# Three norm borders of a two-block transformer kernel: the first unit pair behind each border multiplies rows that have no norm factor yet

## The reference

```
for l in range(DEPTH):                       # DEPTH = 2
    h = rms_norm(x, norm_mix[l])
    z = h @ w_in[l]                          # 2560 columns
    ... attention, gated recurrence and convolution over parts of z ...
    x = x + mix @ w_out[l]
    h = rms_norm(x, norm_mlp[l])
    x = x + jnp.square(jax.nn.relu(h @ w_mlp_in[l])) @ w_mlp_out[l]   # 4096 wide

def rms_norm(x, g):
    y = x * rsqrt(mean(x * x, axis=-1) + EPS)
    return y * g
```

## Time and profile before

| what | value |
|---|---|
| median of 3 runs | 3816.25 us |
| lowest and highest | 3813.84 and 3819.67 us |
| profiled execution | span 3819.2 us from first to last instruction; no time of its own is given for it |
| PE busy | 3654.5 us, 96% |
| DVE busy | 2094.7 us, 55% |
| ACT busy | 1377.0 us, 36% |
| mean granted TensorE clock | 0.974 |

### The profile page before, as it was taken

How to read it: one execution, slowest core, us unless ns; L and a number is a source line. 1 busy time by engine, 2 the same in 40 slices (tenths; PEclk the granted TensorE clock), 3 DMA queues, 4 the chain that set the end, 5 groups by cost and what they waited for, 6 DMA issues and landing times.

```text
span 3819.2 us, 47920 instructions
## 1 busy us (share of the span) xinstructions
PE 3654.5 (96%) x19016; PEld 2946.7 (77%) x19016; DVE 2094.7 (55%) x2735; ACT 1377.0 (36%) x1839; POOL 867.3 (23%) x716
## 2 busy tenths in 40 slices
PE   8988999998899999999899999999989999989998
PEld 6667888766788878886677888788868778778887
DVE  5867443487744454456666435633564655665334
ACT  4764332276433232123663222322233334332222
POOL 2211655321065536552223620000000000000000
PEclk8999999999999999998999999999999999999999
DMA  5212555431265546663234643233322222222331
GB/s 148 78 40 71 149 147 139 100 78 42 68 151 146 137 115 160 145 144 74 52 77 102 162 118 94 77 101 98 99 71 79 72 65 85 63 65 80 101 95 67
DMA packets 564249, 377.75 MB, mean 99 GB/s; under 512 B 37297, under 2 KB 561162, under 8 KB 564026
## 3 DMA queue, kind: packets, MB, share of 16 engines
q1 hardware_dynamic: 564026, 374.69, 37.1%
HBM read 372.45 MB, written 2.17 MB: 98 GB/s over the span
## 4 chain that ended last, share of the span: by engine, by line
PE 79%; DVE 14%; ACT 4%; issue 3%; SPq 0%; DMA 0%; DVEq 0%; ACTq 0%
PE bank L447 62%; PE bank L455 3%; DVE conv_sum L1250 2%; PE bank L493 2%; DVE w_lo L425 2%; PE bank L866 1%; PE bank L487 1%; PE bank L488 1%; DVE norm_tmp L1709 1%; DVE std L928 1%; PE bank L2347 1%; ACT w_hi L416 1%; DVE norm_tmp L1703 1%; DVE X L1705 1%; DVE H_lo L1715 1%
## 5 line engine op out<-in xcount | busy, mean ns | idle before, releaser
L447 PE MATMUL bank<-H_hi,w_hi 128*128 128x512 f32 x2384 | 968.3, 406 | 5.0 <-DVE w_lo L425 1.8
L447 PE MATMUL bank<-H_hi,w_lo 128*128 128x512 f32 x2384 | 932.4, 391 | 0.0
L447 PE MATMUL bank<-H_lo,w_hi 128*128 128x512 f32 x2384 | 931.6, 391 | 0.0
L425 DVE TENSOR_TENSOR w_lo<-w_raw,w_hi 128x2048 fp32r<-128x2048 f32 (+3 forms) x285 | 657.1, 2306 | 148.4 <-ACT w_hi L416 140.7
L416 ACT ACTIVATE w_hi<-w_raw 128x2048 fp32r<-128x2048 f32 (+3 forms) x285 | 529.1, 1857 | 306.4 <-DMA w_raw<-in_ffn_w_up 131.3
L447 PEld LDWEIGHTS bank<-H_hi,w_hi 128*128 128x128 f32 x2384 | 448.3, 188 | 140.6 <-issue 49.0
L526 POOL TENSOR_TENSOR w_mod_raw<-w_mod_raw,silu_c 128x1024 f32<-128x1024 f32 x144 | 283.8, 1971 | 1185.7 <-DMA w_mod_raw<-in_w_mod 1139.6
L447 PE MATMUL bank<-U_hi,w_hi 128*128 128x512 f32 x1376 | 539.4, 392 | 3.7 <-DVE note L985 3.7
L447 PE MATMUL bank<-U_hi,w_lo 128*128 128x512 f32 x1376 | 535.8, 389 | 0.0
L447 PE MATMUL bank<-U_lo,w_hi 128*128 128x512 f32 x1376 | 535.6, 389 | 0.0
L447 PEld LDWEIGHTS bank<-H_hi,w_lo 128*128 128x128 f32 x2384 | 448.1, 188 | 96.7 <-issue 0.3
(11 more groups left out here) (368 smaller groups left out, 4681.1 us busy)
## 6 DMA issues: line engine op xcount, KB each, us to landing
w_mod_raw<-in_w_mod SPq DMA_DIRECT2D x576, 128.0 KB, 5.7
w_raw<-in_ffn_w_gate SPq DMA_DIRECT2D x88, 512.0 KB, 4.0
w_raw<-in_ffn_w_up SPq DMA_DIRECT2D x88, 512.0 KB, 5.5
w_raw<-in_dil_w_in SPq DMA_DIRECT2D x36, 1024.0 KB, 5.1
w_raw<-in_w_mlp_in SPq DMA_DIRECT2D x32, 1024.0 KB, 6.0
w_raw<-in_w_mlp_out SPq DMA_DIRECT2D x32, 1024.0 KB, 5.5
w_raw<-in_ffn_w_down SPq DMA_DIRECT2D x32, 1024.0 KB, 5.0
w_raw<-in_w_in SPq DMA_DIRECT2D x16, 1024.0 KB, 5.5
```

Of the source, the lines that this page charges most:

```text
L425: dve.eng.tensor_tensor(WL[u % SLOTS][:, 0:n], RAW[u % SLOTS][:, 0:n], WH[u % SLOTS][:, 0:n].bitcast(F32), ALU.subtract).then_inc(lo_done. ...
L447: mm = pe.eng.matmul(bank[0:m, :], w[:, k, c0:c0 + m], r[:, k, :], start=(k == 0 and i == 0), stop=(k == kt - 1 and i == 2))
```

## The change

At the three borders, while the last tiles are added to `X`, ACT makes `H_hi` from `X * g` without the factor (`raw_high`) and DVE `H_lo` (`raw_low`). TensorE runs the first pair on these (`pe_raw_pair`) and does the sums of squares behind its third k-step and the spread of the factor behind its fourth. DVE copies the factor out of the bank (`FACTORS`), scales all eight tiles, and ACT and DVE write `H_hi` and `H_lo` again in place, each tile once TensorE has read it (`raw_gone`). The four output tiles of the pair get the factor as DVE reads them out of their banks: for `up` together with the relu, for `z0` in a plain multiplication; ACT did these four before. The units behind the pair wait for the rewritten tiles one by one.

```
+        def pe_raw_pair(pe, u):
...
+            for _, _, place, turn in todo:
+                pe.eng.wait_ge(acc_free[place].sem, turn - 1)
+            for k in range(DT):
+                pe.eng.wait_ge(part_hi.sem, part_hi.next(pe))
+                for wh, wl, place, _ in todo:
+                    pe.eng.matmul(banks[place][:], wh[:, k], rh[:, k, :], start=(k == 0), stop=False)
+                    pe.eng.matmul(banks[place][:], wl[:, k], rh[:, k, :], start=False, stop=False)
+                pe.eng.wait_ge(rhs_ready.sem, rhs_ready.next(pe))
+                for wh, wl, place, _ in todo:
+                    mm = pe.eng.matmul(banks[place][:], wh[:, k], rl[:, k, :], start=False, stop=(k == DT - 1))
...
+                if k == RAW_SUMS:
+                    pe_running_sums(pe)
+                if k == RAW_SPREAD:
+                    pe_spread(pe)
...
+        def raw_high(act, t, gain):
+            act.eng.activation(HH[:, t, :], X[:, t, :], ACT.Identity, scale=gain(t)).then_inc(part_hi.sem, part_hi.add())
...
+        def raw_low(dve, t, gain):
+            dve.eng.wait_ge(part_hi.sem, part_hi.next(dve))
+            dve.eng.scalar_tensor_tensor(HL[:, t, :], X[:, t, :], gain(t), HH[:, t, :].bitcast(F32), ALU.mult, ALU.subtract).then_inc(rhs_ready.sem, rhs_ready.add())
...
+        def scaled_act(act, u):
+            act_std(act, D, True)
+            split_hi(act, u + 2)
+            for t in range(DT):
+                act.eng.wait_ge(scaled.sem, scaled.next(act))
+                raw_gone(act, u, t)
+                act.eng.activation(HH[:, t, :], SC[t % 2][:], ACT.Copy).then_inc(part_hi.sem, part_hi.add())
...
+        def scaled_dve(dve, u, gain, evac):
...
+            split_lo(dve, u + 2)
+            dve.eng.wait_ge(rbc_ready.sem, rbc_ready.next(dve))
+            dve.eng.tensor_copy(FACTORS[:], banks[5][:]).then_inc(rbc_used.sem, rbc_used.add())
...
+            scale(0)
+            for t in range(1, DT):
+                scale(t)
+                rest(t - 1)
+            evac(0)
+            evac(1)
+            rest(DT - 1)
+            evac(2)
+            evac(3)
```

In `last_mix` (borders A and C) the split of the pair's second weight tile moves ahead of the last four adds:

```
-            split_lo(dve, u + AHEAD)
+                if t == 3:
+                    split_lo(dve, u + AHEAD)
+                    raw_low(dve, 0, norm_gain("norm_mlp", l))
+            for t in range(1, DT):
+                raw_low(dve, t, norm_gain("norm_mlp", l))
```

More of the change, by code:

```diff
@@ L290, in add_units, with ahead_of_norm @@
             lin[stage] = range(first, len(units))
+        def ahead_of_norm(stage, third):
+            units[lin[third][0] + (2 if third == stage else 0)]["waits"] = "tiles"
         H, U = (HH, HL), (UH, UL)
@@ L313, in build @@
                 add_units(("down", l, q), U, [square(w2[1024 * q:1024 * q + 1024, :], D, 256 * i) for i in range(4)])
+        for l in range(DEPTH):
+            ahead_of_norm(("up", l, 0), ("up", l, 0))
+        ahead_of_norm(("z0", 1), ("z", 1))
         def add_ffn(l, s):
@@ L822, in evac @@
                 for j in range(2):
-                    bank, free = acc_take(act, u, j)
                     act.eng.wait_ge(mid_used.sem, mid_used.next(act, lag=2))
-                    act.eng.activation(MID[j][:], bank[:], ACT.Relu).then_inc(free.sem, free.add())
-                    act.eng.wait_ge(free.sem, free.made)
+                    if q == 0 and u < lin[("up", l, 0)][2]:
+                        place, turn = acc_place[units[u]["tiles_at"] + j]
+                        act.eng.wait_ge(acc_free[place].sem, turn)
+                    else:
+                        bank, free = acc_take(act, u, j)
+                        act.eng.activation(MID[j][:], bank[:], ACT.Relu).then_inc(free.sem, free.add())
+                        act.eng.wait_ge(free.sem, free.made)
                     act.eng.activation(MID[2 + j][:], MID[j][:], ACT.Square).then_inc(square_r.sem, square_r.add())
@@ L829, in up_act, with up_square, up_raw_dve @@
             return evac
+        def up_square(dve, l, t):
+            dve.eng.wait_ge(square_r.sem, square_r.next(dve))
+            dve.eng.tensor_copy(UH[:, t, :], MID[2 + t % 2][:]).then_inc(dve.step.sem, dve.step.add())
+            dve.eng.wait_ge(dve.step.sem, dve.step.made)
+            dve.eng.tensor_tensor(UL[:, t, :], MID[2 + t % 2][:], UH[:, t, :].bitcast(F32), ALU.subtract).then_inc(rhs_ready.sem, rhs_ready.add())
+            dve.eng.wait_ge(rhs_ready.sem, rhs_ready.made)
+            dve_note(dve, mid_used)
+        def up_raw_dve(dve, l, t):
+            u = lin[("up", l, 0)][t // 2]
+            if t >= 2:
+                up_square(dve, l, t - 2)
+            bank, free = acc_take(dve, u, t % 2)
+            dve.eng.scalar_tensor_tensor(MID[t % 2][:], bank[:], 0.0, FACTORS[:], ALU.max, ALU.mult).then_inc(free.sem, free.add())
+            dve.eng.wait_ge(free.sem, free.made)
         def up_dve(l, q):
@@ L1186, in z_evac, with z_scaled @@
             act.eng.wait_ge(free.sem, free.made)
+        def z_scaled(dve, l, t):
+            bank, free = acc_take(dve, lin[("z0", l)][t // 2], t % 2)
+            dve.eng.tensor_tensor(Z[:, t, :], bank[:], FACTORS[:], ALU.mult).then_inc(free.sem, free.add())
+            dve.eng.wait_ge(free.sem, free.made)
         def head_square(act, t):
@@ L1194, in mixer_act @@
             for t in range(4):
-                z_evac(act, first + t // 2, t % 2, t)
+                if l:
+                    place, turn = acc_place[units[first + t // 2]["tiles_at"] + t % 2]
+                    act.eng.wait_ge(acc_free[place].sem, turn)
+                else:
+                    z_evac(act, first + t // 2, t % 2, t)
             for t in range(4):
```

102 lines of the change are left out of this document (82 added, 20 removed).

## The result

The changed kernel takes 3836.51 us (median of 5 runs, 3832.07 to 3838.36), the kernel before 3816.25 (5 runs beside them, 3805.16 to 3821.88): ratio 1.0048, 95% interval 1.0034 to 1.0063.

What follows compares the result with a forecast made beforehand. The prediction took the time TensorE has no product at the borders as the cost. Its terms, 5.6 us at A, 0.8 at B and 4.1 at C, gave +10.5 on 3816.25: 3827 us, range 3812 to 3838.

Steps and rivals of the forecast that it cites:

- The chain from T to the third unit, T+28.0: From the pair's first matmul to the third unit's at full clock: 28.0 us, the last 3.1 without work for TensorE.
- T: The time of the pair's first matmul at a border, from which the prediction counts the later steps.
- If DVE needs 1.1 us a tile instead of 1.5: Rival: rewriting hidden by the pair, third unit 2.7 us earlier at each border, 3813 or 3810 in all; chance 0.08.
- T at A and C: Pair's first matmul at 343.9 against 346.31 at A, 1011.5 against 1015.50 at C: 2.4 and 4.0 us won.
- T at B: Pair's first matmul at border B at 700.3 against 704.96: 4.7 us won.
- ACT's `w_hi` stands behind the seventh tile's `raw_high`, 0.74 later: Border B, ahead of the pair: the last add to `X` starts at 699.55 instead of 698.81.
- Only the last: Border B: `raw_high` and `raw_low` lie beside products ending 5.4 us apart, so only the last tile costs, 0.74 us.
- The slow start s: Slow clock at the beginning of the pair: 1.5 us at each of borders A and C.
- its bound of 3: Upper bound, in us, on the cost of the slow start at borders A and C; the lower was 0.
- The fourth unit's `w_lo` and the new gap's clock: Stall for late `w_lo`, 1.7 us at A and C each; clock fall behind new gaps, 0.5 there, 1.0 at B.
- The second wait that the prediction wanted to see: Sign: TensorE waits 1 to 3 us at the fourth `up` unit, ended by `w_lo`, casts over 1 us ahead.
- much slower: Rival: DVE stays behind through the `up` units, late `w_lo` stops TensorE: +18 to +25 us, 3838; chance 0.10.

Runs made afterwards that it cites:

- experiment 5: The changed kernel with unused matmuls filling TensorE's gaps ahead of the pair and ahead of the third unit, order unchanged: 3824.92 us, ratio 1.0020.
- Experiment 4: The changed kernel with `raw_low` of each tile behind the next tile's add at border B: 3829.30 us, ratio 1.0040.
- 11: The changed kernel with unused matmuls ahead of the pair alone, the gap before the third unit left as it is: 3824.85 us, ratio 1.0011.
- experiment 9: The changed kernel with `raw_low` behind later adds, sums and spread one k-step earlier, both `w_hi` ahead of the root, fourth unit's `w_lo` after pair read-outs: 3809.09 us, ratio 0.9967.
- experiment 3: The changed kernel with the adds first at A and C, the weight split ahead of them and all `raw_low` behind: 3826.51 us, ratio 1.0031.
- experiment 8: The kernel before the change, with unused matmuls in its gaps behind the last product and behind the spread: 3809.28 us, ratio 0.9986.
- experiment 1: The changed kernel with DVE's read-outs of the pair's first two tiles behind the fifth rewritten tile instead of the seventh: 3841.51 us, ratio 1.0067.
- experiment 2: The changed kernel with the weight splits of the third unit, and at A and C the fourth, ahead of root and reciprocal: 3824.06 us, ratio 1.0026.

## Why the prediction came out as it did

The direction, the place of each wait and the forecast itself held; the loss was under-sized, 10.5 us for 20.4 in the borders. Piece by piece, forecast and measured:

- **The chain from T to the third unit, T+28.0.** Right to 0.2 us, as experiment 5 shows with the clock up (27.94, 27.86, 27.96). Two of its terms were off and cancel: the pair took 24.3 instead of 24.9, and the gap behind it was 3.6 instead of 3.1. "If DVE needs 1.1 us a tile instead of 1.5" is refuted: two scales stand 1.51 apart (366.17, 367.69).
- **T at A and C.** Forecast 6.2 us behind the last product at both (343.9 - 337.70, 1011.5 - 1005.29), measured 6.39 and 6.38. Right.
- **T at B, the step that failed.** "ACT's `w_hi` stands behind the seventh tile's `raw_high`, 0.74 later": it was 2.4 later against the last product. What failed is "Only the last": the tiles ahead of it were given no cost, while `raw_low` locks DVE to ACT, each tile runs 3.77 us in series, and two `raw_low` lost 0.8 and 1.4 us beside GpSimd's bursts. T came 2.8 earlier instead of 4.7: +1.9. Experiment 4 took the lock away and found the pair 1.7 us earlier; in experiment 5, with the lock but without that loss, `w_hi` stood 2.98 ahead of the last product, where the 0.74 of the prediction puts it.
- **The slow start s.** "I take 1.5 us at each, what it cost before", none at B. Measured 2.7, 2.5 and 2.7: +4.9, the largest term. The old cost was that of a slow stretch half hidden in the gap; I carried its price over and not its position. That its bound of 3 was where the truth lay was on the page: the slow window of the earlier trace rows begins before the pair, and the change moves the pair forward into it. Experiments 5 and 11, in which the pair takes 24.3 us at full clock, show that s is the clock's alone.
- **The fourth unit's `w_lo` and the new gap's clock.** Put at 1.7 + 0.5, 1.0, 1.7 + 0.5. Measured 2.8, 2.6 and 2.8. The two overlap: with the clock slow the stall does not show, with the clock up it is 1.8 and 1.9 (experiment 5), as forecast. So 1.7 was right as a stall, and the clock's share was under-sized: +2.8 together. The second wait that the prediction wanted to see, ended by `w_lo`, is not in the changed kernel: there `w_lo` was done at 382.53 and the fourth unit started at 383.74.

The three misses, 4.9 + 2.8 + 1.9, and 0.4 for T at A and C make 10.0, the distance of 10.5 from 20.4 but for rounding. That is in the borders; the time, 18 us by the ratio, is known no better than to a few us. Of the rivals, "much slower" had the size right and the mechanism wrong: the waits of TensorE show none at all in the rest of the first MLP, from the fourth unit of A to the last `down` (317.25 us in both kernels).

The order made the trade a poor one, not the idea. It wins 2 to 4 us ahead of each pair and gives DVE 8 `raw_low` and a second pass over the tiles, and DVE sets the third unit. With the same work in another order (experiment 9) the borders take 124.8 us against 134.1.

What stays open: why the clock fell at C and not at A behind like gaps in experiment 3, and the 3.9 us of experiment 8 that the borders do not show.

## What to carry to other kernels

A gap on TensorE is not paid by its length alone. Ask where the slow stretch behind it will lie: work brought forward into it runs at half speed, and a new short gap can cost nearly as much again in the products behind it (2.6 to 2.8 us behind 3.60 here) as in idle time. Follow a stall that you move to where it lands, and past the end of your table (experiment 1). When a start moves forward, list what the helper engine must do until the next bank is read, and put first what is next on the chain (here sums, reciprocal, `w_lo` of the next unit), last what has slack. And run the kernel before with its gaps filled too: 6.5 us were to be had here by that alone, where the best order without filling gave 8.9.

## What the runs showed of the hardware that was not expected

- At A the granted clock stood at 0.50 for 6.82 us both times begun in the gap: in one of 8.61 us with 3.3 us of short matmuls in it, and in one of 6.39 us with none.
- It fell in a third unit behind 3.60 us of idling, and in experiment 2 behind 2.26 us at B and C, but not at A.
- Unused matmuls in the gap at A (5.61 us busy out of 6.41) kept it at 1.00, at no cost to the work beside them: DVE's adds and ACT's squares ended when they had.
- While small matmuls were woven between products it stayed low longest: 17 us of the stretch from third to fourth unit of B in experiment 1, 5.6 us there in the changed kernel, none in the kernel before.
- Beside GpSimd's burst DVE's cast took 1.29 us and the subtraction 1.68, against 0.43 and 0.69 alone. The Trainium skill ("SBUF — State Buffer", "Who interferes with whom") has the two exclude each other on a shared port pair; by that rule DVE loses what is left of each GpSimd operation that it meets, and the row of the cast agrees nearly: it started at 373.39 with 1.0 us left of an operation of 1.90 (from 372.50), and lost 0.9.
